# Time steps of the state-space layer with tokens on partitions, and their running sums as products with a triangle of ones

## The chip, the cores and the metric

The kernel runs on one core of a Trainium2 chip. The metric is the device time of one execution in microseconds. Before the change the median of three runs is 2298.25 us (2295.49 to 2298.49).

## The reference, cut to what matters

The program is a three-layer network on 512 tokens with 1024 features. The second layer's mixer is a state-space layer with 8 groups of 4 heads, so 32 heads. What the change touches is the step size of each token and head, and its running sum:

```
z, xbc, dt_raw = split(h @ w_in)                    # dt_raw: 512 tokens x 32 heads
dt = softplus(dt_raw + dt_bias)
a  = -exp(a_log)                                    # one value a head
cs = cumsum(dt * a) along the tokens                # inside a block of tokens
decay[l, s] = exp(cs[l] - cs[s]) for l >= s         # and, between blocks, with the block's end added
y  = (C B^T * decay) @ (x * dt) + d_skip * x
```

## The kernel before

All matrix products against weights are made in three parts: a weight chunk (128x1024) is loaded by SyncE into a ring of four buffers `raw`, ScalarE rounds it to `whi` (L1044), GpSimd takes `raw - whi` as `wlo` (L504), and TensorE multiplies `whi` and `wlo` with the high and low parts of the activations. One output tile is 24 products of 512 columns (L543, `single`). It goes to one of banks 0 to 3 in turn, so a tile waits until the tile four places before it has been read (`bank_free`).

The order of the work on each engine is written out by hand. In the state-space layer tile 0 of `m_in` holds `dt_raw` with the 32 heads on 32 partitions and the tokens along the free dimension. Tiles 1 to 4 are the x (two), B and C of group 0; VectorE runs a four-tap convolution over each (`conv(0, s)`, L1650 and L1652), ScalarE the silu (`conv_silu`, L1195). Tiles 5 and 6 are the gates of group 0. The first four tiles are computed together (`four("m_in", 2)`, L566 and L570), tiles 4 to 6 one after another in the loop at L807. Then `m_body(g)` computes for each group the six tiles of the next group, and between them turns x to token-major (`ssd_turn`), forms B times C (`ssd_cb`), and multiplies with the decays (`ssd_y`).

Before the first `m_body` VectorE works out the time steps (L1759 to L1784): bias, the exponent from ScalarE (L1186), a series for log(1+e), then the running sums of `-exp(a_log) * dt` by scans (L1780 inside each of four blocks of 128 tokens, L1782 from the end of a block over the rest), all as 32x512 tiles in SBUF with heads on partitions. `conv(0, 0)`, `conv(0, 1)` and `conv(0, 2)` stand between these operations. The result `cs` (32x1280) is written to memory (L468) and read back row by row, broadcast to 128 partitions, as `csb` (L463). SyncE does that after it has issued the load of chunk 12 of `m_in`, which itself waits until chunk 8 has been split. TensorE transposes `cs` and `dt` to token-major (L812, L813), VectorE copies these out as `cs_tok`, `ncs_tok`, `dt_tok` (L1876 to L1878), and all engines wait on `tok_ready` before the first `m_body`. `conv(0, 3)` comes after that wait.

A step wrapped in `step(...)` is waited for by VectorE itself before the next instruction.

Of the kernel before, what the change touches and what calls it, by code (L numbers as in the profile page):

```python
# [40 lines left out]
HEADS = GROUPS * HPG  # L41
# [45 lines left out]
T0, _ = starts(TILES)  # L87
# [36 lines left out]
def program(nc, io):  # L124
    with ExitStack() as ctx:
        def sem(name):
            return ctx.enter_context(nc.semaphore(name))

        def sb(name, shape, dt=F32):
            return ctx.enter_context(nc.sbuf_tensor(name, shape, dt))  # L130
# [13 lines left out]
        epscol = sb("epscol", [P, 1])  # L144
        dtp = sb("dtp", [HEADS, 4])
        acc = sb("acc", [P, S])
# [7 lines left out]
        ident = kst[:, K0["ident"]:K0["ident"] + P]  # L154
        tri = kst[:, K0["tri"]:K0["tri"] + P]
# [9 lines left out]
        def view(at, name, shape, dt=F32):  # L165
            with ExitStack() as v:
                if at:
                    v.enter_context(nc.sbuf_tensor(f"pad_{name}", [P, at // 4], F32))
                return v.enter_context(nc.sbuf_tensor(name, shape, dt))

        KB = 1024
        H = 0
        G = 32 * KB
# [25 lines left out]
        sums_m = view(G + 16 * KB, "sums_m", [P, 3, S])  # L199
        dts = view(G + 24 * KB, "dts", [HEADS, 7, S])  # L200
        cs = view(G + 76 * KB, "cs", [HEADS, PACK])
# [46 lines left out]

        dt_lin, dt_exp, a_exp, cs_ready, cs_out, tokT_done, tok_ready = (
            sem(n) for n in ("dt_lin", "dt_exp", "a_exp", "cs_ready", "cs_out", "tokT_done", "tok_ready"))  # L250
        grp_ready, xT_done, xdt_done, cb_done, cbm_dve, cbm_act = (
# [92 lines left out]
        def _(sp):  # L344
# [28 lines left out]
            sp.dma_start(kst[:], io["kst"]).then_inc(kst_in, 16)  # L373
            sp.dma_start(dtp[:, 0:2], io["dtp"]).then_inc(kst_in, 16)
            sp.dma_start(x[:], io["x"].rearrange("p (k n) -> p k n", k=KD)).then_inc(x_in, 16)
# [155 lines left out]
        def _(pe):  # L531
# [259 lines left out]
            def out_part(m, first, last):  # L791
# [12 lines left out]
                if last % CH == 0:  # L804
                    mm.then_inc(chunk_done, 1)

            for s in range(3, GSTEP):  # L807
                single("m_in", 1 + s, wait=False)

            pe.wait_ge(cs_ready, 1)  # L810
            for i in range(NT):
                nc.tensor.transpose(psum[4][:, i * HEADS:(i + 1) * HEADS], cs[:, i * P:(i + 1) * P], ident[0:HEADS, 0:HEADS])  # L812
                mm = nc.tensor.transpose(psum[5][:, i * HEADS:(i + 1) * HEADS], dts[:, 6, i * P:(i + 1) * P], ident[0:HEADS, 0:HEADS])  # L813
            mm.then_inc(tokT_done, 1)
            pe.wait_ge(tok_ready, 3)
            for g in range(GROUPS - 1):
# [218 lines left out]
        def _(act):  # L1035
# [147 lines left out]
            act.wait_ge(kst_in, 32)  # L1183
            nc.scalar.activation(dtp[:, 2:3], dtp[:, 1:2], ACT.Exp).then_inc(a_exp, 1)
            act.wait_ge(dt_lin, 1)
            nc.scalar.activation(dts[:, 1, :], dts[:, 0, :], ACT.Exp).then_inc(dt_exp, 1)  # L1186

# [74 lines left out]
            for s in range(GSTEP):  # L1262
# [4 lines left out]
                split_next(0, s)  # L1267
            act.wait_ge(tok_ready, 3)
            for g in range(GROUPS - 1):
# [211 lines left out]
        def _(dve):  # L1481
# [264 lines left out]
            def conv(G, s):  # L1746

                t = T0["m_in"] + 1 + GSTEP * G + s
                done(C0["m_in"] + 1 + GSTEP * G + s)
                if 4 * G + s >= 2:  # L1750

                    dve.wait_ge(grp_ready, 4 * G + s - 1)
                taps(tb[:, s % 2, :], psum[t % 4][:], "m_conv", 4 * G + s, 4, bank_free[t % 4])
# [3 lines left out]
            b = T0["m_in"] % 4  # L1757
            X, EXP, SERIES, SQUARE, SUM, MAX, DT = range(7)
            step(TS(dts[:, SUM, :], psum[b][0:HEADS, :], dtp[:, 0:1], None, ALU.add))  # L1759
            STT(out=dts[:, X, :], in0=dts[:, SUM, :], scalar=-1.0, in1=dts[:, SUM, :], op0=ALU.mult, op1=ALU.min).then_inc(dt_lin, 1)  # L1760
            TS(dts[:, MAX, :], dts[:, SUM, :], 0.0, None, ALU.max).then_inc(bank_free[b], 1)
            conv(0, 0)
            dve.wait_ge(dt_exp, 1)
            step(TS(dts[:, SERIES, :], dts[:, EXP, :], 2.0, None, ALU.add))
            step(nc.vector.reciprocal(dts[:, SERIES, :], dts[:, SERIES, :]))
            step(TT(dts[:, SERIES, :], dts[:, EXP, :], dts[:, SERIES, :], ALU.mult))
            conv(0, 1)
            step(TT(dts[:, SQUARE, :], dts[:, SERIES, :], dts[:, SERIES, :], ALU.mult))
            step(TS(dts[:, SUM, :], dts[:, SQUARE, :], 1.0 / 17, None, ALU.mult))
            for odd in range(15, 1, -2):  # L1770
                step(STT(out=dts[:, SUM, :], in0=dts[:, SUM, :], scalar=1.0 / odd, in1=dts[:, SQUARE, :], op0=ALU.add, op1=ALU.mult))
            step(STT(out=dts[:, SUM, :], in0=dts[:, SUM, :], scalar=1.0, in1=dts[:, SERIES, :], op0=ALU.add, op1=ALU.mult))
            step(STT(out=dts[:, DT, :], in0=dts[:, SUM, :], scalar=2.0, in1=dts[:, MAX, :], op0=ALU.mult, op1=ALU.add))
            dve.wait_ge(a_exp, 1)
            step(TS(dts[:, X, :], dts[:, DT, :], dtp[:, 2:3], -1.0, ALU.mult, ALU.mult))
            step(nc.vector.memset(dts[:, EXP, :], 1.0))

            for i in range(NT):
                at = slice(i * P, (i + 1) * P)
                step(nc.vector.tensor_tensor_scan(cs[:, at], dts[:, EXP, at], dts[:, X, at], 0.0, ALU.mult, ALU.add))  # L1780
            for i, (at, n) in OFF_COL.items():
                last = nc.vector.tensor_tensor_scan(cs[:, at:at + n], dts[:, EXP, (i + 1) * P:S], dts[:, X, (i + 1) * P:S],  # L1782
                                                    cs[:, (i + 1) * P - 1:(i + 1) * P], ALU.mult, ALU.add)
            last.then_inc(cs_ready, 1)  # L1784
            conv(0, 2)

# [86 lines left out]

            dve.wait_ge(tokT_done, 1)
            by_token = lambda bank: bank[:, 0:P].rearrange("p (i h) -> p i h", i=NT)
            nc.vector.tensor_copy(cs_tok[:], by_token(psum[4])).then_inc(tok_ready, 1)  # L1876
            TS(ncs_tok[:], by_token(psum[4]), -1.0, None, ALU.mult).then_inc(tok_ready, 1)
            nc.vector.tensor_copy(dt_tok[:], by_token(psum[5])).then_inc(tok_ready, 1)  # L1878
            dve.wait_ge(tok_ready, 3)
            conv(0, 3)  # L1880
# [251 lines left out]
def layout(a):  # L2132
# [14 lines left out]
    ins["kst"] = np.concatenate([np.eye(P), np.triu(np.ones((P, P))), qvalid, emask], axis=1).astype(np.float32)  # L2147
    ins["dtp"] = np.stack([a["m_dt_bias"][0], a["m_a_log"][0]], axis=1)
    ins["x"] = moving(a["x"][0].T)
# [56 lines left out]
```

## Time and profile before

| | before |
|---|---|
| median of 3 runs | 2298.25 us |
| profiled execution | 2297.04 us, its span 2295.2 us |
| TensorE busy | 2223.1 us, 97% |
| VectorE busy | 1242.6 us, 54% |
| ScalarE busy | 994.1 us, 43% |
| GpSimd busy | 974.2 us, 42% |
| mean granted TensorE clock | 0.978 |

The span is from the first to the last instruction that the profiler recorded. Busy shares are means over stages. Starts in the rows below are microseconds from the start of the span, and durations are microseconds unless marked ns. A matrix product's duration includes its way through the array, so products overlap; the distance between two starts is the rate.

### The profile page before, as it was taken

The page shows a single profiled execution, that of the slowest core. Times are in us where ns is not written, and L with a number is a line of the kernel's source. Part 1 is how long each engine was busy: PE and PEld are TensorE (multiplying, and loading weights), DVE is VectorE, ACT ScalarE, POOL GpSimd, SP SyncE. Part 2 cuts the span into 40 slices and gives each one's busy share as a digit, 9 for nine tenths or more (in the row PEclk, how much of TensorE's full clock was granted, in tenths as well). Part 3 has the DMA queues.
Part 4 walks back from the last instruction along what each step waited for, and adds up shares of the span by engine and source line. Part 5 has one row for each costly group of instructions (what it writes and reads, how often), then busy time and mean ns, then how long its engine had stood idle before and what let it go on. Part 6 is the DMA issues. An engine that isn't in the chain of part 4 may idle for free.

```text
span 2295.2 us, 28959 instructions
## 1 busy us (share of the span) xinstructions
PE 2223.1 (97%) x10434; PEld 1761.0 (77%) x10434; DVE 1242.6 (54%) x1718; ACT 994.1 (43%) x1420; POOL 974.2 (42%) x421
## 2 busy tenths in 40 slices
PE   6999999999979999989999999999999899999998
PEld 4788888788867777767788888878677688888886
DVE  5876666521297787786522221250777755666412
ACT  4324443333435546554534334453555634444332
POOL 3544443446534333334444446556211143444563
PEclk8999899999989999999899999999999999999999
DMA  7553475553315344332133223334321032333232
GB/s 304 212 202 125 152 265 201 185 143 95 115 40 186 111 142 149 113 111 90 59 103 97 91 72 95 109 106 145 97 67 47 29 107 76 108 93 91 76 91 72
DMA packets 74096, 273.83 MB, mean 119 GB/s; under 512 B 8519, under 2 KB 11207, under 8 KB 67736
## 3 DMA queue, kind: packets, MB, share of 16 engines
q1 hardware_dynamic: 70632, 266.74, 35.6%
q10 hardware_dynamic: 3376, 5.90, 0.8%
q8 instruction: 57, 0.93, 0.2%
q14 instruction: 31, 0.25, 0.0%
HBM read 269.21 MB, written 8.12 MB: 121 GB/s over the span
## 4 chain that ended last, share of the span: by engine, by line
PE 76%; issue 14%; POOL 5%; DVE 3%; ACT 1%; DMA 0%; ACTq 0%; POOLq 0%; SPq 0%; DVEq 0%
PE bank L543 60%; POOL wlo L504 5%; PE bank L913 4%; PE bank L566 2%; PE bank L1006 2%; PE bank L970 1%; PE bank L934 1%; PE bank L953 1%; PE bank L570 1%; PE bank L607 1%; PE bank L615 1%; PE bank L654 1%; PE bank L854 0%; DVE x L1553 0%; DMA ada_first<-ada_d 0%
## 5 line engine op out<-in xcount | busy, mean ns | idle before, releaser
L504 POOL TENSOR_TENSOR wlo<-raw,whi 128x1024 fp32r<-128x1024 f32 x382 | 928.8, 2438 | 1235.9 <-ACT whi L1044 1235.7
L1044 ACT ACTIVATE whi<-raw 128x1024 fp32r<-128x1024 f32 x382 | 401.3, 1055 | 622.9 <-PE bank L543 588.3
L543 PE MATMUL bank<-h_hi,whi 128*128 128x512 f32 x1616 | 649.3, 402 | 4.9 <-DVE dt_tok L1878 2.5
L543 PE MATMUL bank<-h_hi,wlo 128*128 128x512 f32 x1616 | 638.1, 395 | 0.0
L543 PE MATMUL bank<-h_lo,whi 128*128 128x512 f32 x1616 | 636.0, 394 | 0.0
L543 PEld LDWEIGHTS bank<-h_hi,whi 128*128 128x128 f32 x1616 | 303.9, 188 | 79.6 <-issue 5.7
L543 PEld LDWEIGHTS bank<-h_hi,wlo 128*128 128x128 f32 x1616 | 303.8, 188 | 77.2
L543 PEld LDWEIGHTS bank<-h_lo,whi 128*128 128x128 f32 x1616 | 304.0, 188 | 70.4
L543 PE MATMUL bank<-g_hi,whi 128*128 128x512 f32 x592 | 236.3, 399 | 0.0
L543 PE MATMUL bank<-g_hi,wlo 128*128 128x512 f32 x592 | 233.2, 394 | 0.0
L543 PE MATMUL bank<-g_lo,whi 128*128 128x512 f32 x592 | 232.1, 392 | 0.0
L1713 DVE TENSOR_TENSOR tb<-ta,bank 128x512 f32<-128x512 f32 x44 | 30.1, 685 | 222.3 <-PE bank L543 202.7
L1495 DVE TENSOR_TENSOR g_lo<-tb,g_hi 128x512 f32 (+1 forms) x52 | 109.1, 2098 | 51.9 <-ACT g_hi L1173 45.0
L543 PEld LDWEIGHTS bank<-g_hi,wlo 128*128 128x128 f32 x592 | 111.1, 188 | 29.1
L543 PEld LDWEIGHTS bank<-g_lo,whi 128*128 128x128 f32 x592 | 111.1, 188 | 26.4
L543 PEld LDWEIGHTS bank<-g_hi,whi 128*128 128x128 f32 x592 | 111.1, 188 | 25.4
L1511 DVE TENSOR_TENSOR sums<-sums,sq 128x512 f32<-128x512 f32 x21 | 14.5, 692 | 193.2 <-ACT sq L1107 193.1
L1652 DVE SCALAR_TENSOR_TENSOR tb<-bank,vec,tb 128x511 f32<-128x511 f32 (+1 forms) x140 | 104.8, 749 | 9.8
L566 PE MATMUL bank<-h_hi,whi 128*128 128x512 f32 x160 | 68.2, 426 | 9.2 <-ACT h_hi L1089 7.0
L1843 DVE TENSOR_TENSOR csb<-csb,cbm 128x1280 f32<-128x1280 f32 x32 | 72.0, 2288 | 0.3
L519 POOL TENSOR_TENSOR h_lo<-tb,h_hi 128x512 fp32r<-128x512 f32 x35 | 45.2, 1293 | 59.9 <-ACT tb L1090 59.6
L566 PE MATMUL bank<-h_hi,wlo 128*128 128x512 f32 x160 | 67.2, 420 | 0.0
(337 smaller groups left out, 2953.5 us busy)
## 6 DMA issues: line engine op xcount, KB each, us to landing
raw<-f_in_d SPq DMA_DIRECT2D x88, 512.0 KB, 3.5
raw<-m_d SPq DMA_DIRECT2D x65, 512.0 KB, 3.7
ada_f<-ada_d SPq DMA_DIRECT2D x24, 1024.0 KB, 7.0
raw<-g_in_d SPq DMA_DIRECT2D x44, 512.0 KB, 3.5
raw<-w_in_d SPq DMA_DIRECT2D x41, 512.0 KB, 3.6
csb<-cs_d SPq DMA_DIRECT2D x32, 640.0 KB, 6.5
ada_a<-ada_d SPq DMA_DIRECT2D x16, 1024.0 KB, 4.9
raw<-a_in_d SPq DMA_DIRECT2D x24, 512.0 KB, 6.0
```

The costliest lines, as they stand in the source:

```text
L504: nc.gpsimd.tensor_tensor(wlo[:, s], raw[:, s], whi[:, s].bitcast(F32), ALU.subtract).then_inc(lo_ready, 1)
L519: nc.gpsimd.tensor_tensor(h_lo[:, k, :], tb[:, k % 2, :], h_hi[:, k, :].bitcast(F32), ALU.subtract).then_inc(in_ready, 1)
L543: mm = nc.tensor.matmul(psum[bank][:], w[:, s, kk, :], xs[part == "lo"][:, k, :], start=first and kk == 0 and i == 0, stop=last and kk == ...
L566: nc.tensor.matmul(psum[tiles[i]][:], w[:, (C0[name] + i) % RING, k, :], h_hi[:, k, :], start=k == 0 and j == 0, stop=False)
L570: mm = nc.tensor.matmul(psum[tiles[i]][:], whi[:, (C0[name] + i) % RING, k, :], h_lo[:, k, :], start=False, stop=k == KD - 1)
L913: mm = nc.tensor.matmul(psum[7][:], w[:, c % RING, m // 3, :], (h_hi, h_lo)[part == "lo"][:, m // 3, :], start=m == 0, stop=m == 23)
L1006: mm = nc.tensor.matmul(psum[b][:], w[:, c % RING, k, :], (h_hi, h_lo)[part == "lo"][:, k, :], start=kk == 0 and i == 0, stop=kk == 3 and ...
L1044: nc.scalar.activation(whi[:, s], raw[:, s], ACT.Copy).then_inc(hi_ready, 1)
L1495: TT(dst, whole, hi.bitcast(F32), ALU.subtract).then_inc(in_ready, 1)
L1652: ins = STT(out=out[:, d:S], in0=src[:, 0:S - d], scalar=col(width - 1 - d), in1=out[:, d:S], op0=ALU.mult, op1=ALU.add)
L1713: TT(tb[:, j % 2, :], ta[:, j % 2, :], psum[b][:], ALU.mult).then_inc(bank_free[b], 1)
L1843: TT(csb[:, r, :], csb[:, r, :], cbm[:], ALU.mult).then_inc(m_done, 1)
```

## The change

The 32x512 product `dt_raw` is copied out of its bank at once and turned by four transposes to 128 tokens by 4x32 (block, head), all before tile 4. Bias, exponent, series and the product with `-exp(a_log)` are then made on 128x128 tiles, with one operand of each in PSUM in most of them; `dt_tok` is now their direct result. For that the parameters `dtp` are loaded broadcast to 128 partitions. The running sums are five fp32 products with the triangle of ones `tri`, issued after tile 5: one gives `cs` with tokens on partitions, four give it with heads on partitions. The sums from a block's end over later blocks are the in-block sums plus the end, or plus two or three ends that are added first. The whole series stands between `conv(0, 0)` and `conv(0, 1)`, where it stood on both sides of `conv(0, 1)`. The transposes at L812 and L813 and the copies at L1876 to L1878 go away, and the wait for the token-major values comes before `conv(0, 2)`.

```diff
-        dtp = sb("dtp", [HEADS, 4])
+        dtp = sb("dtp", [P, 2, HEADS])
...
-        dts = view(G + 24 * KB, "dts", [HEADS, 7, S])
+        dts = view(G + 24 * KB, "dts", [HEADS, S])
+        dtt = view(G + 26 * KB, "dtt", [P, 6, NT, HEADS])
+        ends = view(G + 29 * KB, "ends", [HEADS, 4])
...
-            sp.dma_start(dtp[:, 0:2], io["dtp"]).then_inc(kst_in, 16)
+            sp.dma_start(dtp[:].rearrange("p a h -> p (a h)"), io["dtp"].broadcast_to([P, 2 * HEADS])).then_inc(kst_in, 16)
...
+            b = T0["m_in"] % 4
+            pe.wait_ge(bank_free[b], T0["m_in"] // 4 + 1)
+            for i in range(NT):
+                mm = nc.tensor.transpose(psum[4][:, i * HEADS:(i + 1) * HEADS], dts[:, i * P:(i + 1) * P], ident[0:HEADS, 0:HEADS])
+            mm.then_inc(dt_turn, 1)
             for s in range(3, GSTEP):
                 single("m_in", 1 + s, wait=False)
-
+                if s == 4:
+                    pe.wait_ge(dta_out, 1)
+                    nc.tensor.matmul(psum[4][:, P:2 * P], tri, dtt[:, 5].rearrange("p i h -> p (i h)"), start=True, stop=True)
+                    for i in range(NT):
+                        mm = nc.tensor.matmul(psum[5][0:HEADS, i * P:(i + 1) * P], dtt[:, 5, i, :], tri, start=True, stop=True)
+                    mm.then_inc(cs_sum, 1)
+            pe.wait_ge(tok_ready, 2)
             pe.wait_ge(cs_ready, 1)
-            for i in range(NT):
-                nc.tensor.transpose(psum[4][:, i * HEADS:(i + 1) * HEADS], cs[:, i * P:(i + 1) * P], ident[0:HEADS, 0:HEADS])
-                mm = nc.tensor.transpose(psum[5][:, i * HEADS:(i + 1) * HEADS], dts[:, 6, i * P:(i + 1) * P], ident[0:HEADS, 0:HEADS])
-            mm.then_inc(tokT_done, 1)
-            pe.wait_ge(tok_ready, 3)
...
-            nc.scalar.activation(dtp[:, 2:3], dtp[:, 1:2], ACT.Exp).then_inc(a_exp, 1)
+            nc.scalar.activation(psum[6][:, 0:HEADS], dtp[:, 1, :], ACT.Exp).then_inc(a_exp, 1)
             act.wait_ge(dt_lin, 1)
-            nc.scalar.activation(dts[:, 1, :], dts[:, 0, :], ACT.Exp).then_inc(dt_exp, 1)
+            nc.scalar.activation(psum[5][:, P:2 * P], dtt[:, 0].rearrange("p i h -> p (i h)"), ACT.Exp).then_inc(dt_exp, 1)
...
-            step(TS(dts[:, SUM, :], psum[b][0:HEADS, :], dtp[:, 0:1], None, ALU.add))
-            STT(out=dts[:, X, :], in0=dts[:, SUM, :], scalar=-1.0, in1=dts[:, SUM, :], op0=ALU.mult, op1=ALU.min).then_inc(dt_lin, 1)
-            TS(dts[:, MAX, :], dts[:, SUM, :], 0.0, None, ALU.max).then_inc(bank_free[b], 1)
+            nc.vector.tensor_copy(dts[:], psum[b][0:HEADS, :]).then_inc(bank_free[b], 1)
...
+            dve.wait_ge(dt_turn, 1)
+            linear = by_head(psum[4][:, 0:P])
+            step(TT(SUM_P, linear, bias, ALU.add))
+            step(TT(SUM, linear, bias, ALU.add))
+            step(TS(MAX_P, SUM, 0.0, None, ALU.max))
+            STT(out=X, in0=SUM_P, scalar=-1.0, in1=SUM, op0=ALU.mult, op1=ALU.min).then_inc(dt_lin, 1)
             conv(0, 0)
             dve.wait_ge(dt_exp, 1)
+            step(TS(DENOM, EXP_P, 2.0, None, ALU.add))
+            step(nc.vector.reciprocal(DENOM, DENOM))
+            step(TT(SERIES, EXP_P, DENOM, ALU.mult))
+            step(nc.vector.tensor_copy(SER_P, SERIES))
+            SQUARE_P = SUM_P
+            step(TT(SQUARE_P, SER_P, SERIES, ALU.mult))
+            step(TS(SUM, SQUARE_P, 1.0 / 17, None, ALU.mult))
+            for odd in range(15, 1, -2):
+                step(STT(out=SUM, in0=SUM, scalar=1.0 / odd, in1=SQUARE_P, op0=ALU.add, op1=ALU.mult))
+            step(STT(out=SUM, in0=SUM, scalar=1.0, in1=SER_P, op0=ALU.add, op1=ALU.mult))
+            step(STT(out=dt_tok[:], in0=SUM, scalar=2.0, in1=MAX_P, op0=ALU.mult, op1=ALU.add))
+            dve.wait_ge(a_exp, 1)
+            rate = psum[6][:, 0:HEADS].unsqueeze(1).broadcast_to([P, NT, HEADS])
+            STT(out=DTA, in0=rate, scalar=-1.0, in1=dt_tok[:], op0=ALU.mult, op1=ALU.mult).then_inc(dta_out, 1)
             conv(0, 1)
...
-            for i in range(NT):
-                at = slice(i * P, (i + 1) * P)
-                step(nc.vector.tensor_tensor_scan(cs[:, at], dts[:, EXP, at], dts[:, X, at], 0.0, ALU.mult, ALU.add))
+            dve.wait_ge(cs_sum, 1)
+            nc.vector.tensor_copy(cs_tok[:], by_head(psum[4][:, P:2 * P])).then_inc(tok_ready, 1)
+            TS(ncs_tok[:], by_head(psum[4][:, P:2 * P]), -1.0, None, ALU.mult).then_inc(tok_ready, 1)
+            step(nc.vector.tensor_copy(cs[:, 0:S], psum[5][0:HEADS, :]))
+            end = [cs[:, (i + 1) * P - 1:(i + 1) * P] for i in range(3)] + [ends[:, i:i + 1] for i in range(3)]
+            for i, (a, c) in enumerate(((0, 1), (1, 2), (3, 2))):
+                step(TS(end[3 + i], end[a], end[c], None, ALU.add))
             for i, (at, n) in OFF_COL.items():
-                last = nc.vector.tensor_tensor_scan(cs[:, at:at + n], dts[:, EXP, (i + 1) * P:S], dts[:, X, (i + 1) * P:S],
-                                                    cs[:, (i + 1) * P - 1:(i + 1) * P], ALU.mult, ALU.add)
+                for j in range(i + 1, NT):
+                    first = {(0, 1): 0, (1, 2): 1, (2, 3): 2, (0, 2): 3, (1, 3): 4, (0, 3): 5}[i, j]
+                    col = at + (j - i - 1) * P
+                    last = TS(cs[:, col:col + P], cs[:, j * P:(j + 1) * P], end[first], None, ALU.add)
+                    if (i, j) != (1, 3):
+                        step(last)
             last.then_inc(cs_ready, 1)
+            dve.wait_ge(tok_ready, 2)
             conv(0, 2)
```

## Rows read from the trace of the kernel before

**Rows 1.** The page: busy time, share of the span, instructions.
```profile
PE 2223.1 (97%) x10434; PEld 1761.0 (77%) x10434; DVE 1242.6 (54%) x1718; ACT 994.1 (43%) x1420; POOL 974.2 (42%) x421
```

**Rows 2.** TensorE's waits, 640 to 760 us: total, times, longest.
```profile
PE bank L812 <- DVE cs L1782: 8.4, 1, 8.4
PE bank L543 <- DVE dt_tok L1878: 2.5, 1, 2.5
PE bank L543 <- DVE dts L1761: 1.0, 1, 1.0
```

**Rows 3.** Timeline of TensorE: start, duration, instruction, idle before and its releaser.
```profile
658.20 0.50 PE L543 MATMUL bank<-h_hi,whi 128*128 128x512 f32 x1 [1.05 <-DVE dts L1761]
...
687.21 0.79 PE L543 MATMUL bank<-h_hi,whi 128*128 128x512 f32 x1 [2.53 <-DVE dt_tok L1878]
...
694.59 1.03 PE L734 MATMUL bank<-kst,xg 128*128 128x128 f32 x8
...
714.56 2.39 PE L768 MATMUL bank<-csb,xdt 128*64 128x128 f32 x28
...
779.72 1.12 PE L727 MATMUL bank<-sq,ones 128*128 128x512 f32 x2 [0.55 <-DVE sq L1801]
```

**Rows 4.** Stretches: length, PE, PEld, DVE, ACT, POOL busy, then PEclk, DMA.
```profile
675.30:683.60 8.30, 0.00 (x0) 0.00 (x0) 7.79 (x15) 0.00 (x0) 0.00 (x0) 0.62 0.14 55
...
687.20:691.10 3.90, 3.89 (x10) 3.07 (x11) 2.99 (x4) 1.84 (x4) 2.38 (x1) 0.53 0.00 0
...
1809.00:1812.00 3.00, 1.78 (x18) 1.28 (x18) 2.93 (x7) 2.69 (x7) 0.00 (x0) 0.74 0.00 0
```

**Rows 5.** Timeline of VectorE.
```profile
654.17 0.74 DVE L1759 TENSOR_SCALAR dts<-bank,dtp 32x512 f32<-32x512 f32 x1 [2.42 <-PE bank L570]
...
658.08 0.73 DVE L1650 TENSOR_SCALAR tb<-bank,vec 128x512 f32<-128x512 f32 x1
...
665.92 0.75 DVE L1650 TENSOR_SCALAR tb<-bank,vec 128x512 f32<-128x512 f32 x1
...
668.94 0.67 DVE L1768 TENSOR_TENSOR dts<-dts 32x512 f32<-32x512 f32 x1
...
686.48 0.28 DVE L1876 COPY cs_tok<-bank 128x128 f32<-128x128 f32 x1
686.68 0.28 DVE L1877 TENSOR_SCALAR ncs_tok<-bank 128x128 f32<-128x128 f32 x1
...
705.65 3.50 DVE L1843 TENSOR_TENSOR csb<-csb,cbm 128x1280 f32<-128x1280 f32 x2
```

**Rows 6.** Single lines: durations in ns, shortest/median/longest, first and last start.
```profile
L1652 DVE SCALAR_TENSOR_TENSOR tb<-bank,vec,tb x140: 746/748/752, 658.8 to 2161.6; 128x511 f32<-128x511 f32 x54, 128x510 f32<-128x510 f32 x54, 128x509 f32<-128x509 f32 x32
...
L1652 DVE SCALAR_TENSOR_TENSOR tb<-ta,vec,tb x16: 749/750/2771, 61.6 to 180.5; 128x511 f32<-128x511 f32 x8, 128x510 f32<-128x510 f32 x8
...
L1828 DVE TENSOR_SCALAR csb<-csb,cs_tok x128: 269/277/589, 699.2 to 1008.0; 128x128 f32<-128x128 f32 x128
...
L1979 DVE TENSOR_SCALAR stat<-stat x48: 168/169/2331, 1614.9 to 1810.1; 128x2 f32<-128x2 f32 x48
...
L1765 DVE RECIPROCAL dts<-dts x1: 3341/3341/3341, 661.5 to 661.5; 32x512 f32<-32x512 f32 x1
...
L741 PE MATMUL bank<-cg,bg x64: 271/275/275, 701.1 to 1007.2; 128*128 128x128 f32 x64
```

**Rows 7.** Timeline of GpSimd.
```profile
655.36 2.51 POOL L504 TENSOR_TENSOR wlo<-raw,whi 128x1024 fp32r<-128x1024 f32 x1 [5.03 <-ACT whi L1044]
...
670.80 2.95 POOL L504 TENSOR_TENSOR wlo<-raw,whi 128x1024 fp32r<-128x1024 f32 x1 [5.46 <-ACT whi L1044]
```

**Rows 8.** Timeline of SyncE's queue.
```profile
691.12 0.43 SPq L468 DMA_DIRECT2D cs_d<-cs  x1
694.95 2.00 SPq L463 DMA_DIRECT2D csb<-cs_d  x4
```

**Rows 9.** Timeline of ScalarE, first decay row of group 0.
```profile
699.20 1.31 ACT L1211 ACTIVATE csb<-csb,ncs_tok 128x384 f32<-128x384 f32 x3 [1.96 <-DMA csb<-cs_d]
```

More of the change, by code:

```diff
@@ L247, in program @@
         gate_out, prod_out, conv_out = sem("gate_out"), sem("prod_out"), sem("conv_out")
-        dt_lin, dt_exp, a_exp, cs_ready, cs_out, tokT_done, tok_ready = (
-            sem(n) for n in ("dt_lin", "dt_exp", "a_exp", "cs_ready", "cs_out", "tokT_done", "tok_ready"))
+        dt_turn, dt_lin, dt_exp, a_exp, dta_out, cs_sum, cs_ready, cs_out, tok_ready = (
+            sem(n) for n in ("dt_turn", "dt_lin", "dt_exp", "a_exp", "dta_out", "cs_sum", "cs_ready", "cs_out", "tok_ready"))
         grp_ready, xT_done, xdt_done, cb_done, cbm_dve, cbm_act = (
@@ L469, in _ @@
             sp.wait_ge(cs_out, 16)
-            sp.wait_ge(tok_ready, 3)
+            sp.wait_ge(tok_ready, 2)
             for f in range(2):
@@ L1267, in _ @@
                 split_next(0, s)
-            act.wait_ge(tok_ready, 3)
+            act.wait_ge(tok_ready, 2)
             for g in range(GROUPS - 1):
@@ L1757, in _ @@
             b = T0["m_in"] % 4
-            X, EXP, SERIES, SQUARE, SUM, MAX, DT = range(7)
-            step(TS(dts[:, SUM, :], psum[b][0:HEADS, :], dtp[:, 0:1], None, ALU.add))
-            STT(out=dts[:, X, :], in0=dts[:, SUM, :], scalar=-1.0, in1=dts[:, SUM, :], op0=ALU.mult, op1=ALU.min).then_inc(dt_lin, 1)
-            TS(dts[:, MAX, :], dts[:, SUM, :], 0.0, None, ALU.max).then_inc(bank_free[b], 1)
+            nc.vector.tensor_copy(dts[:], psum[b][0:HEADS, :]).then_inc(bank_free[b], 1)
+            by_head = lambda t: t.rearrange("p (i h) -> p i h", i=NT)
@@ new lines, in _ @@
+            SUM_P, EXP_P, SER_P, MAX_P = (by_head(psum[5][:, i * P:(i + 1) * P]) for i in range(4))
+            X, SUM, SERIES, DENOM, DT, DTA = (dtt[:, i] for i in range(6))
+            bias = dtp[:, 0, :].unsqueeze(1).broadcast_to([P, NT, HEADS])
+            dve.wait_ge(dt_turn, 1)
[4 more added lines that the diff above has]
+            STT(out=X, in0=SUM_P, scalar=-1.0, in1=SUM, op0=ALU.mult, op1=ALU.min).then_inc(dt_lin, 1)
@@ L1762, in _ @@
             conv(0, 0)
             dve.wait_ge(dt_exp, 1)
-            step(TS(dts[:, SERIES, :], dts[:, EXP, :], 2.0, None, ALU.add))
-            step(nc.vector.reciprocal(dts[:, SERIES, :], dts[:, SERIES, :]))
-            step(TT(dts[:, SERIES, :], dts[:, EXP, :], dts[:, SERIES, :], ALU.mult))
-            conv(0, 1)
[L1768 to L1776, printed above, removed]
-            for i in range(NT):
-                at = slice(i * P, (i + 1) * P)
-                step(nc.vector.tensor_tensor_scan(cs[:, at], dts[:, EXP, at], dts[:, X, at], 0.0, ALU.mult, ALU.add))
@@ L1872, in mixed @@
                     lo_part(m_lo[:, k, :], y32[:, k, :], m_hi[:, k, :], I0["m_out"] + k)
[L1874 to L1879, printed above, removed]
             conv(0, 3)
@@ L2147, in layout @@
     ins["kst"] = np.concatenate([np.eye(P), np.triu(np.ones((P, P))), qvalid, emask], axis=1).astype(np.float32)
-    ins["dtp"] = np.stack([a["m_dt_bias"][0], a["m_a_log"][0]], axis=1)
+    ins["dtp"] = np.concatenate([a["m_dt_bias"][0], a["m_a_log"][0]])[None]
     ins["x"] = moving(a["x"][0].T)
```

## The prediction, made before the changed kernel was built or run

> **What bounds the kernel now.** I read the page first. TensorE is busy 97% of the span and the others about half [rows 1], so over the whole kernel time is won only where TensorE stands still or runs slowly. The second view is TensorE's waits in the stretch that the change touches: 8.4 us for the last scan of the running sums, then 2.5 us for the copy of `dt_tok`, and 1.0 us earlier for the bank that L1761 frees [rows 2]. The third is TensorE's timeline. Tile 4 starts at 658.20, three tiles of 24 products follow at one product per 0.233 us (a tile is 5.7 us with its first gap), and they are through at 675.1. Then TensorE has only eight small transposes until 687.21, when the first tile of `m_body(0)` starts. That tile ends at 694.59 and the next begins behind the eight transposes of `ssd_turn`, at 695.4 [rows 3]. The stretches tell the rest: in 675.3 to 683.6 the mean granted clock is 0.62, which means the clock fell to 1.2 GHz about 2 us after TensorE had stopped, and until 691.1 it is 0.53 [rows 4]. Nine products there start 0.43 us apart instead of 0.233, so the low level costs 1.7 us after the wait. The hole is about 12 us of missing work and 1.7 us of slow work, and VectorE is what ends it: its series and scans run without a pause.
>
> I use one mark for the sum, the start of the second tile of `m_body(0)`: 695.4 before.
>
> **Step 1, bank and turn.** The copy of `dt_raw` takes the place of L1759 at 654.17 (0.74 us) [rows 5], so the bank is free at 654.9 rather than after L1761. Tile 4 then waits only for GpSimd's chunk, which ends at 657.87 [rows 7], and starts at 657.9, 0.3 us earlier. The four transposes issue after TensorE's last product of the four tiles (657.0) at 0.13 us each, as the eight at 694.59 [rows 3]. They lie inside that same wait and cost nothing; without that cover, 0.5 us. VectorE gets their result at 657.7.
>
> **Step 2, the 128x128 operations.** The trace has copies out of PSUM of this size at 0.28 us [rows 5] and a scalar operation in SBUF of 0.277 [rows 6]; with the 0.04 us that a waited step adds, I take 0.32 us each. Bounds: 0.20 us, the start distance of the two copies at 686.48 with no wait between, and 0.75 us, the 512-wide forms. The reciprocal of 512 elements takes 3.34 us [rows 6]; a quarter and the fixed part of the 2-wide operations (0.17) give 0.98. Four operations end at 659.0. `conv(0, 0)` takes its 3.0 us, to 662.0, 0.9 us later than before. Then 16 operations, 15 at 0.32 and the reciprocal: 5.8 us, to 667.8. None of them reads two SBUF tensors. Such forms never lengthened in 140 cases (746 to 752 ns), where the form with two SBUF inputs goes to 2771 [rows 6], so GpSimd's pieces beside them cost nothing; if they do count, that is a rival below. ScalarE's exponent (0.3 us) and the chunk behind it come 2 us later; chunk 5 is then split at 662.8, and tile 5 needs it at 663.6.
>
> A rule that speaks against the step is in the Trainium skill, VectorE: DVE Perf Modes, section "The TRN2 errata": a PSUM source costs 62 cycles more of fixed part than an SBUF one. By that the series would be an estimated 1 us longer. The trace has no such difference at this size (0.28 against 0.277), so the sum doesn't hold it.
>
> **Step 3, conv(0, 1) behind the whole series.** Before, it ran at 665.92 to 668.94 [rows 5], just in time for tile 6, which takes its bank. Now it runs 667.8 to 670.8. TensorE ends tile 5 at 669.2, makes the five fp32 products (ten records, as L741's are two records each [rows 6], 1.3 us at 0.13) until 670.5 and starts tile 6 at 670.9. The products lie in the wait for the bank; uncovered they cost 1.3 us. Tile 6 ends at 676.6, 1.5 us later than before.
>
> **Step 4, the sums out of PSUM.** After 670.8: two copies (0.2 each), the 32x512 copy (0.74), three sums of ends (0.20 each) to 672.6, and six 32x128 additions (0.31 each): 674.4 if nothing else happens. But these nine are scalar operations with input and output in SBUF. Such operations stretch when GpSimd is in a piece: L1979 from 169 to 2331 ns, L1828 from 277 to 589 [rows 6]. GpSimd's next piece starts 1.86 us after `conv(0, 1)` ends (668.94 to 670.80 before [rows 5, 7]), so at 672.7, for 2.4 us. I let one addition pass; five wait to 675.2 and end at 676.8. Bounds of this wait: 0 and 2.4 us, and I take the upper one, because the piece is released by the same `conv(0, 1)` as the additions.
>
> **Step 5, the start of m_body(0).** Its first tile takes the bank of `conv(0, 2)`, which is now queued behind the additions on VectorE: 676.8 to 679.8. So TensorE waits 3.2 us, 676.6 to 679.8. The old gap shows the clock falling after about 2 us, the sparse work of 1809 to 1812 lowers it too (0.74) [rows 4]; I take the fall and the same 1.7 us. Bounds: 0 and 1.7, or 4.7 if a whole tile runs slowly. First tile 679.8 to 687.2, transposes 0.8, mark at 688.0. Gain at the mark: 7.4 us. `conv(0, 3)` and its silu are done at 683.5, chunk 8 at 684.0, both in time.
>
> **Step 6, the decay rows.** They don't gain as much. `cs` is written once load 12 has gone, and that waits for chunk 8: 690.72 before, when `cs` had long been ready, and 684.0 now. 0.4 us on, the write's 3.8 us and 4.2 us to the first row [rows 8, 9] put it at 692.4, 4.4 us behind the mark, before 3.8. The first group has the room: the products that need its first decays began at 714.56, those decays were done at 709.1 [rows 3, 5]. ScalarE and VectorE run 0.6 us later against TensorE through group 0, and the square sum of that group, which already misses by 0.55 us in later groups [rows 3], can miss by 0.3 in the first: cost 0.3 us. Bounds: 0 and 2.4, one GpSimd piece in front of it.
>
> Nothing else moves: the broadcast of `dtp` is 32 KB at the start in the shadow of the first loads.
>
> **Sum.** 7.4 - 0.3 = 7.1 us. The profiled execution of 2297.04 us (span 2295.2 and 1.8 around it) becomes 2289.9. The median of the runs is 1.2 us above the profiled one, so 2291.1 is the median I forecast. What is late next is `conv(0, 2)`, that is VectorE behind GpSimd.
>
> **Rivals.**
> The additions escape GpSimd (0.18): `conv(0, 2)` ends at 677.4, TensorE waits 0.8 us, the clock stays, mark at 684.0, which is 11.4 us earlier. The rows then lag 2.4 us more and cost about 1.2 at the first square sum. 10.2 us gained, 2288.0. For it: half of a 2 us interval decides. Against: both start from one event.
>
> The clock stays high in a wait of 3.2 us (0.17): mark 9.1 us earlier, lag 2.3 us, cost 1.2: 2290.3, the same answer.
>
> Late pieces add up (0.17): the square sum meets a full piece (2.4), the low clock lasts two more products (0.4): gain 4.6, 2293.6.
>
> The series waits for GpSimd in spite of its PSUM operands (0.08): the pieces for chunks 5 and 6 lie in it, up to 2.2 us each, gain 2.7, 2295.5. Against it are 140 rows without one case.
>
> The lag of group 0 stays (0.06): if VectorE can't regain the 2.4 us, each of seven groups repeats it, 16.8 us against 9.1 gained, 7.7 us slower: 2306. It decides from 1.3 us a group. For it: TensorE already waits on VectorE once a group [rows 3]. Against: VectorE is busy about 33 us of each 43 us group, so it has 10 us to catch up.
>
> **How the numbers follow.** My forecast has 0.34. With the rival that gives the same time it holds half. A measurement of this kernel can tell about 0.2% (4.6 us) from no change. Faster by more than that: the forecast, the two next to it and the first rival, and half of the late pieces, 0.79; within it: 0.14; slower: 0.07. The range reaches from 2285.5 (first rival, and no cost at the square sum) to 2295.5.
>
> **What would show it.** In the profile after: four transposes before 658 and tile 4 at 657.9; series of 128x128 operations at 0.32 us without a 2 us one; tile 6 at 670.9 behind a wait for `conv(0, 1)`; one addition of over 2 us, beside a GpSimd piece; TensorE's wait of about 3 us for `conv(0, 2)` with a clock under 1.0 behind it; the mark near 688; no new wait after the first square sum. The forecast is wrong if the series takes over 8 us, if the additions don't stretch, or if any group after the second starts with a larger wait than 0.55 us.

## The result: 39.8 us faster, about four fifths of it outside the changed code

The changed kernel takes 2258.55 us (median of 4 runs, 2257.73 to 2260.74) against 2298.37 us for the kernel before (4 runs). The ratio is 0.9832, with a 95% interval of 0.9819 to 0.9844. The forecast was 2291.1 with a range of 2285.5 to 2295.5, so the result is 27 us below the range. The profiled execution has a span of 2255.9 us against 2295.2. In the spans, that is 39.3 us less. One execution of e12 below took 2447.12 us at a mean granted clock of 0.84; it moves that median by 0.01 us, and no other was slow.

I read the profile after in the same order. First the busy line, then TensorE's waits from 630 to 1110 us, which is the whole state-space stage and more than the stretch of [rows 2], as total, times, longest:

```profile
PE 2185.6 (97%) x10440; PEld 1758.1 (78%) x10440; DVE 1229.8 (55%) x1722; ACT 993.5 (44%) x1420; POOL 975.6 (43%) x421
```

```profile
PE bank L729 <- DVE sq L1827: 11.7, 6, 6.7
PE bank L545 <- DVE tb L1660: 3.3, 2, 3.0
PE bank L545 <- POOL wlo L506: 1.8, 2, 1.4
```

In the kernel before, the square sums (L727 there) waited as follows between the same times:

```profile
PE bank L727 <- DVE sq L1801: 8.9, 6, 6.3
```

The wait of 8.4 us for the scans and that of 2.5 us for `dt_tok` [rows 2] are gone, and the forecast wait of about 3 us for `conv(0, 2)` has come (L1660). The square sums wait 2.8 us more in all. The busy line holds the surprise: TensorE has six more instructions than before, and is busy 37.5 us less (2185.6 against 2223.1 [rows 1]). Waits that go away don't make the work itself shorter.

TensorE's timeline of the stage: the four transposes, tile 4, the products with the triangle, tile 6, the first tile of `m_body(0)`, the transposes behind it, and the square sum of group 1:

```profile
648.48 0.43 PE L812 MATMUL bank<-kst,dts 32*128 32x32 f32 x4
649.34 0.47 PE L545 MATMUL bank<-h_hi,whi 128*128 128x512 f32 x1 [0.42 <-POOL wlo L506]
...
660.41 0.38 PE L818 MATMUL bank<-dtt,kst 128*128 128x128 f32 x2
660.72 1.06 PE L820 MATMUL bank<-kst,dtt 128*32 128x128 f32 x8
662.03 0.50 PE L545 MATMUL bank<-h_hi,whi 128*128 128x512 f32 x1 [0.24 <-DVE tb L1660]
...
670.83 0.47 PE L545 MATMUL bank<-h_hi,whi 128*128 128x512 f32 x1 [3.03 <-DVE tb L1660]
...
676.41 1.04 PE L736 MATMUL bank<-kst,xg 128*128 128x128 f32 x8
...
761.04 1.12 PE L729 MATMUL bank<-sq,ones 128*128 128x512 f32 x2 [1.00 <-DVE sq L1827]
```

Tile 4 starts at 649.34 and not at 658.20 [rows 3]. Of these 8.86 us, 8.56 are won before the first changed instruction of the series: the copy of `dt_raw` starts at 645.61 (below), and the instruction in its place started at 654.17 [rows 5]. That is the part that my prediction does not have. It becomes visible when one reads the distance between starts of products in a place without waits. The mean over all neighbouring 512-column products (some 7950 distances between 205 and 260 ns) is 233.4 ns before and 229.0 ns after, in every stage of the program alike. A stage that the change doesn't touch shows it in two rows: from the first sums after the short convolution to the sums after the first feed-forward block there are 1584 such products. The first block is the kernel before, the second the kernel after.

```profile
226.88 2.73 PE L607 MATMUL bank<-ones,sums 128*128 128x1 f32 x24
...
623.12 2.73 PE L607 MATMUL bank<-ones,sums 128*128 128x1 f32 x24
```

```profile
225.48 2.74 PE L609 MATMUL bank<-ones,sums 128*128 128x1 f32 x24
...
615.06 2.73 PE L609 MATMUL bank<-ones,sums 128*128 128x1 f32 x24
```

396.24 us against 389.58: 6.66 us less, or 4.2 ns for each of 1584 products.

Inside the stage of the series things went almost as forecast. VectorE's timeline after (the copy of `dt_raw`, the first of the four operations, the seven terms of the series, the sums, `conv(0, 2)`), then GpSimd's piece, SyncE's queue and ScalarE's first decay row:

```profile
645.61 0.68 DVE L1766 COPY dts<-bank 32x512 f32<-32x512 f32 x1 [2.10 <-PE bank L572]
648.95 0.30 DVE L1773 TENSOR_TENSOR bank<-bank,dtp 128x128 f32<-128x128 f32 x1 [2.67 <-PE bank L812]
...
653.47 0.95 DVE L1780 RECIPROCAL dtt<-dtt 128x128 f32<-128x128 f32 x1
...
655.78 2.21 DVE L1787 SCALAR_TENSOR_TENSOR dtt<-dtt,bank 128x128 f32<-128x128 f32 x7
...
658.88 0.74 DVE L1658 TENSOR_SCALAR tb<-bank,vec 128x512 f32<-128x512 f32 x1
...
664.01 2.62 DVE L1806 TENSOR_SCALAR cs<-cs,ends 32x128 f32<-32x128 f32 x2
666.66 0.59 DVE L1806 TENSOR_SCALAR cs<-cs 32x128 f32<-32x128 f32 x2
...
667.49 0.73 DVE L1658 TENSOR_SCALAR tb<-bank,vec 128x512 f32<-128x512 f32 x1
```

```profile
663.76 2.48 POOL L506 TENSOR_TENSOR wlo<-raw,whi 128x1024 fp32r<-128x1024 f32 x1 [6.32 <-ACT whi L1052]
```

```profile
675.17 0.43 SPq L470 DMA_DIRECT2D cs_d<-cs  x1
679.13 1.98 SPq L465 DMA_DIRECT2D csb<-cs_d  x4
```

```profile
683.27 1.31 ACT L1219 ACTIVATE csb<-csb,ncs_tok 128x384 f32<-128x384 f32 x3 [3.81 <-DMA csb<-cs_d]
```

And the granted clock behind TensorE's wait (length, busy of PE, PEld, DVE, ACT, POOL, then PEclk, DMA):

```profile
667.00:671.20 4.20, 1.17 (x6) 0.69 (x5) 4.06 (x7) 0.59 (x1) 0.00 (x0) 1.00 0.41 125
671.20:675.00 3.80, 3.80 (x18) 3.13 (x17) 2.28 (x4) 2.46 (x5) 2.42 (x1) 1.00 0.00 0
```

It stayed at 2.4 GHz, where the longer hole of before had lowered it [rows 4]. That is so in this execution; in most later ones of the same series it fell, as the section on the prediction shows.

### The profile page after: what moved, and what is told of

Same layout as the page of the kernel before. It is cut to its first block, busy times and chain, and to the rows that moved or that the text cites. A ratio compares the mean times of both kernels' runs of the same rounds, so it can differ in the third digit from the quotient of the medians.

```text
span 2255.9 us, 28975 instructions
## 1 busy us (share of the span) xinstructions
PE 2185.6 (97%) x10440; PEld 1758.1 (78%) x10440; DVE 1229.8 (55%) x1722; ACT 993.5 (44%) x1420; POOL 975.6 (43%) x421
## 4 chain that ended last, share of the span: by engine, by line
PE 76%; issue 14%; POOL 5%; DVE 3%; ACT 1%; DMA 0%; ACTq 0%; POOLq 0%; SPq 0%; DVEq 0%
PE bank L545 60%; POOL wlo L506 5%; PE bank L921 4%; PE bank L568 2%; PE bank L1014 2%; PE bank L978 1%; PE bank L942 1%; PE bank L572 1%; PE bank L961 1%; PE bank L656 1%; PE bank L617 1%; PE bank L609 1%; PE bank L862 1%; DVE x L1561 0%; DMA x<-x_d 0%
## 5 line engine op out<-in xcount | busy, mean ns | idle before, releaser
L545 PE MATMUL bank<-h_hi,whi 128*128 128x512 f32 x1616 | 639.7, 396 | 5.1 <-DVE tb L1660 3.3
L545 PE MATMUL bank<-g_hi,whi 128*128 128x512 f32 x592 | 230.9, 390 | 0.0
L1660 DVE SCALAR_TENSOR_TENSOR tb<-bank,vec,tb 128x511 f32<-128x511 f32 (+1 forms) x140 | 104.9, 749 | 9.8
L568 PE MATMUL bank<-h_hi,whi 128*128 128x512 f32 x160 | 67.5, 422 | 8.9 <-ACT h_hi L1097 7.0
```

Of the source, the lines that this page charges most:

```text
L545: mm = nc.tensor.matmul(psum[bank][:], w[:, s, kk, :], xs[part == "lo"][:, k, :], start=first and kk == 0 and i == 0, stop=last and kk == ...
L568: nc.tensor.matmul(psum[tiles[i]][:], w[:, (C0[name] + i) % RING, k, :], h_hi[:, k, :], start=k == 0 and j == 0, stop=False)
L1660: ins = STT(out=out[:, d:S], in0=src[:, 0:S - d], scalar=col(width - 1 - d), in1=out[:, d:S], op0=ALU.mult, op1=ALU.add)
```

## What moved without being named in the change

`dtp` grew from 4 to 64 floats a partition (16 to 256 bytes). SBUF addresses are handed out in the order of the tensors, and a tensor takes a multiple of 32 bytes in this program. So every tensor behind `dtp` moved up by 224 bytes: `acc` from 86848 to 87072, and all views with the moving operands of the large products (`h_hi`, `h_lo`, `g_hi`, `g_lo`, `m_hi`, `mg_hi` and so on) from 105440 to 105664. Modulo 256 the views go from 224 to 192. The weights `whi` and `wlo` are allocated earlier and stay at 128. Within these tensors all steps are multiples of 512 bytes, so one number holds for all products.

Each large product has two operands in SBUF: a block of weights (`whi` or `wlo`), which a weight load of its own (PEld in the profile) brings in, and 512 columns of activations, here called the moving operand. Theory A: the start address of the moving operand sets the pace. Theory B: something in the changed code does. Theory C came up after the first runs: the distance between moving operand and weights, modulo 256, sets it.

## The experiments

**Moving the tiles by 32 or 64 bytes.** Four kernels, each one line in front of `acc`:

```diff
+        sb("gap", [P, 8])       # e1, e3: 32 bytes
+        sb("gap", [P, 16])      # e2, e4: 64 bytes
         acc = sb("acc", [P, S])
```

> The kernel before with an unused tensor of 32 bytes a partition in front of acc and nothing else: all later tiles lie 32 bytes higher, so that the moving operands of the large products (h_hi, g_hi and the rest) start at a multiple of 64 bytes instead of 32 above one, as they do in the changed kernel. Theory A (the start address of the moving operand sets the pace of the products: 0.233 us a product before, 0.229 after): about 30 us faster than before, near 2268, products 0.229 us apart everywhere. Theory B (the 30 us outside the stretch of the series come from something in the changed code itself): the same time as before, 2298, products 0.233 apart.

> The kernel before with an unused tensor of 64 bytes a partition in front of acc: all later tiles move by 64 bytes, the moving operands still start 32 above a multiple of 64. Theory A in its form with 64-byte multiples: the same as before, 2298, products 0.233 us apart. If any move of the tiles or a multiple of 128 or 256 were what counts, it would be 10 to 30 us faster. Theory B: the same.

> The changed kernel with an unused tensor of 32 bytes a partition in front of acc: the moving operands start 32 bytes above a multiple of 64 again. Theory A: the 30 us are lost and only the gain of the series is left, 9 us against before: 2289, products 0.233 us apart. Theory B: 2258.5 as the changed kernel.

> The changed kernel with an unused tensor of 64 bytes a partition in front of acc: the moving operands start at a multiple of 256 bytes instead of at 192 above one. Theory A with 64-byte multiples: 2258.5, as the changed kernel. If larger multiples count further: faster than that, at most by another 30 us (products 0.225 us apart). Theory B: 2258.5.

Measured (kernel before beside them: 2296.67 us): e1 2290.47 (ratio 0.9961 to 0.9982), e2 2301.86 (1.0017 to 1.0040), e3 2290.64 (0.9966 to 0.9985), e4 2281.24 (0.9914 to 0.9948). The brackets are 95% intervals of the ratio to it. Theory B falls: an unused tensor of 32 bytes takes 32 of the 40 us back (e3), and the old program gets slower with one of 64 bytes, where theory A too had expected no change. Theory A holds in its kind but not in its form: multiples of 64 bytes are not the rule, since e1 has one and gains 6 us only, and e4 has one and is 23 us slower than the changed kernel. The paces pair up across the two programs: 233.4 ns for before and e3, both at 224; 232.6 and 232.4 for e1 and e4, both at 0.

**Which address.** e5 moves only the weights, e6 only the second region of views, e7 only the scratch tiles, and e8 all later tiles by 128 bytes.

```diff
+        csil = sb("csil", [P, KD])          # e5: 32 bytes, moved here from behind mod
         raw = sb("raw", [P, RING, CH, P])
...
-        G = 32 * KB                         # e6
+        G = 32 * KB + 32
...
+        ssum = sb("ssum", [P, NT])          # e7: 32 bytes, moved here from behind root
         acc = sb("acc", [P, S])
...
+        sb("gap", [P, 32])                  # e8
         acc = sb("acc", [P, S])
```

> The changed kernel with the 32-byte tensor csil moved in front of raw: raw, whi, wlo and x lie 32 bytes higher, everything from ncol on (all moving operands) stays. Theory A (the pace of a product follows from the start address of the moving operand alone; so far 233.35 ns at 224 modulo 256, 229.0 at 192, 232.4 at 0, 234.25 at 32, in either kernel): 229.0 ns a product and 2258. Theory C (it follows from the distance between the moving operand and the weights that are loaded meanwhile): another pace, 230 to 234, and 2265 to 2300. Theory B (no address matters): 2258.

> The changed kernel with only the second region of views moved up by 32 bytes (G = 32 KB + 32): h_hi and h_lo stay at 192 modulo 256, g_hi, g_lo, m_lo, mg_hi and mg_lo go to 224. Theory A: inside one execution products with h_hi and h_lo stay at 229.0 ns and products with g_hi, g_lo and mg go to 233.35, so about 2400 slower products by 4.4 ns, 10 us: 2268. Theory B (one pace for a whole program, set by anything but the operand's address): all products alike.

> The kernel before with ssum (32 bytes) moved in front of acc: acc, modacc, sq, rstd, ta, tb and root lie 32 bytes higher, the views with the moving operands of the large products stay at 224 modulo 256. Theory A: 233.35 ns a product and 2297, the kernel before. If the place of the scratch tiles, which VectorE, ScalarE and GpSimd use, were the cause: 232.4 ns and 2290 as in the gap of 32 bytes.

> The changed kernel with an unused tensor of 128 bytes a partition in front of acc: the moving operands start at 64 modulo 256, which is 64 modulo 128 as in the changed kernel. Theory A with a period of 128 bytes: 229.0 ns, 2258. With a period of 256 bytes or with the distance to the weights modulo 256 as its argument: another pace between 228 and 235 ns, and about 7.8 us for each ns.

Measured: e5 2290.95, e6 2269.24, e7 2298.75 (one run), e8 2291.05 us. e7 leaves the pace at 233.4: the scratch tiles have no part in it. e6 shows the address most clearly, because it has both paces in one execution. Twice two starts 24 products apart, first with `h_hi` (192 modulo 256), then with `g_hi` (224):

```profile
2024.71 0.39 PE L545 MATMUL bank<-h_hi,whi 128*128 128x512 f32 x1
...
2030.20 0.39 PE L545 MATMUL bank<-h_hi,whi 128*128 128x512 f32 x1
...
2134.70 0.39 PE L545 MATMUL bank<-g_hi,whi 128*128 128x512 f32 x1
...
2140.30 0.39 PE L545 MATMUL bank<-g_hi,whi 128*128 128x512 f32 x1
```

5.49 and 5.60 us, 229 and 233 ns a product; the means over the execution are 229.1 with `h` and 233.3 with `g`. But e5 refutes theory A: no moving operand moved, only the weights by 32 bytes, and the pace went from 229.0 to 233.3 and 32 us were lost. e8 (233.3 ns) rules out a period of 128 bytes. Theory C had allowed both paces, but had no value of its own for either distance yet, so it needed a test.

**The distance.** e9 gives the kernel before the distance 64 by moving the weights instead of the views, e10 tries the distance 0. e11 belongs to the stage of the series (below), e12 is the changed kernel again.

```diff
+        csil = sb("csil", [P, KD])          # e9, in the kernel before
         raw = sb("raw", [P, RING, CH, P])
...
+        sb("gap", [P, 48])                  # e10, in the changed kernel
         acc = sb("acc", [P, S])
```

> The kernel before with the 32-byte tensor csil moved in front of raw, no instruction changed: the weights whi and wlo start at 160 modulo 256, the moving operands stay at 224, so their distance is 64 as in the changed kernel (192 and 128). Theory C (the pace follows from that distance modulo 256: 64 gives 229.0 ns, 96 gives 233.35, 128 gives 232.4, 160 gives 234.25, 32 and 192 give 233.3): 229.0 ns and 2297 less 30, so 2267, without any part of the change. Theory A (the moving operand's address alone): 233.35 and 2297. A third form, in which both addresses count by themselves: another pace.

> The changed kernel with an unused tensor of 192 bytes a partition in front of acc: moving operands and weights both start at 128 modulo 256, distance 0, which no run had. Theory C has no value for it; the values so far lie between 229.0 and 234.25 ns, so 2258 to 2297; below 229.0 it would be a faster kernel than the changed one, by 7.8 us for each ns. Theory A: a value of its own for the address 128.

Measured (kernel before beside them: 2298.01): e9 2268.58 (ratio 0.9856 to 0.9889), e10 2248.59 (0.9765 to 0.9804). e9 has no changed instruction, the moving operands at their old addresses, and the pace of the changed kernel, 229.0 ns. Its two rows for the feed-forward block stand 389.6 us apart like those after. So addresses alone give 29.4 us, of the 36.8 that the changed kernel gains beside the same runs (e12 below, 2261.19). e10 is faster than the changed kernel by 10 us, at 226.7 ns with `g` and 227.3 with `h`. That is less than my 7.8 us for each ns. The state-space stage is why: between the sums before and behind it (the rows of L607 or L609) it takes 468.54 us in e10 and 465.35 after. The granted clock fell behind TensorE's wait in e10 and not after, and the first tile of `m_body(0)` took 8.31 us instead of 5.58.

**Distance 0 at another address, the missing distance, and both gains together.**

```diff
+        sb("gap0", [P, 8])                  # e15, in the kernel before
         raw = sb("raw", [P, RING, CH, P])
...
+        sb("gap", [P, 40])                  # e15 and e14 (e14 in the changed kernel)
         acc = sb("acc", [P, S])
```

> The kernel before with unused tensors of 32 bytes in front of raw and 160 bytes in front of acc, no instruction changed: weights and moving operands both start at 160 modulo 256, distance 0. Theory C: 226.8 ns a product as at 128 and 128, and a time near the changed kernel without any of its instructions, 2297 less 30 less 10, so 2258. If the absolute addresses count besides the distance: another pace.

> The changed kernel with a gap of 160 bytes in front of acc: moving operands at 96, weights at 128 modulo 256, distance 224, the one multiple of 32 that no run had. Theory C has no value for it; the other odd multiples of 32 gave 233.3 (32), 233.35 (96) and 234.25 (160), so 233 to 234.5 ns and 2288 to 2297 are likely if the pattern holds.

Measured (kernel before beside them: 2296.16): e15 2252.64 (0.9793 to 0.9823), e14 2289.92 (0.9961 to 0.9981). e15 has weights and moving operands at 160 where e10 has them at 128, and the same pace to 0.1 ns: the distance decides, not the place. It is also 6 us faster than the changed kernel, and has not one of its changed instructions.

All runs in one table, but for e6, which has the distances 64 and 96 in one program (229.1 and 233.3 ns; 2269.24 us). Distance is the address of the moving operand less that of the weights, modulo 256; the pace is the mean time between starts, over all large products of the one profiled execution of each:

| distance | pace, ns | kernels (median us) |
|---|---|---|
| 0 | 227.2 | e10 (2248.59), e15 (2252.64), e13 (2242.88) |
| 32 | 233.3 | e5 (2290.95) |
| 64 | 229.0, e12 229.5 | after (2258.55), e9 (2268.58), e11 (2258.85), e12 (2261.19) |
| 96 | 233.4 | before, e3 (2290.64), e7 (2298.75) |
| 128 | 232.4 to 232.6 | e4 (2281.24), e1 (2290.47) |
| 160 | 234.3 | e2 (2301.86) |
| 192 | 233.3 | e8 (2291.05) |
| 224 | 233.3 | e14 (2289.92) |

**The gain of the series by itself.** Pairs with equal distance differ in the series and not in the pace:

> The changed kernel once more on the chip that runs e9 and e11: 2258.5, 229.0 ns a product. Against e9, which has the same pace and the old series, it gives the gain of the series alone: 7.1 us by the forecast, 9 us by the marks in the profile after. Against e11 it gives the price of the wait for conv(0, 2).

e12 measured 2261.19 (0.9816 to 0.9855), so 7.4 us less than e9, measured beside it. The other pairs measured side by side give 9.2 (e1 less e4) and 6.0 (before less e3); e15 less e10, not side by side, gives 4.1. The forecast was 7.1. The traces allow a closer look, at the state-space stage alone, from the sums in front of it to those behind it:

| distance | old series, us | new series, us | gain | first tile of `m_body(0)`, new series |
|---|---|---|---|---|
| 96 | before 477.52 | e3 471.31 | 6.2 | 7.22 us |
| 128 | e1 480.05 | e4 472.60 | 7.5 | 8.43 us |
| 0 | e15 475.89 | e10 468.54 | 7.4 | 8.31 us |
| 64 | e9 475.05 | after 465.35, e12 465.49 | 9.7, 9.6 | 5.58 us, 5.60 us |

The series gains most where its first tile is not slowed by a lower clock. Two microseconds of a single stage are scatter, though: e7 took 479.85 with the distance and the series of before.

**The wait for conv(0, 2).** e11 takes away what forms it, by another order of the instructions:

```diff
             step(nc.vector.tensor_copy(cs[:, 0:S], psum[5][0:HEADS, :]))
+            dve.wait_ge(tok_ready, 2)
+            conv(0, 2)
             ...
             last.then_inc(cs_ready, 1)
-            dve.wait_ge(tok_ready, 2)
-            conv(0, 2)
...
             pe.wait_ge(tok_ready, 2)
-            pe.wait_ge(cs_ready, 1)
```

> The changed kernel with conv(0, 2) in front of the sums of ends and the six additions, and without TensorE's wait for cs_ready (tok_ready stays; the decay rows still wait for cs_ready). No tile moves. If the additions behind GpSimd's piece are what keeps TensorE waiting 3.03 us before m_body(0): conv(0, 2) starts at 663.0 instead of 667.5, that wait is gone, and the time is 3 us below the changed kernel, 2255.5. If the decay rows or the square sum of group 0 take over: 0 to 1 us below it.

Measured 2258.85 (4 runs, 2254.47 to 2264.41), 2.3 us below e12, measured beside it, with ranges that overlap: not told apart by the times. The trace shows what happened. TensorE's waits in e11 from 620 to 760 us, of 0.4 us and more:

```profile
PE bank L568 <- ACT h_hi L1096: 1.8, 1, 1.8
PE bank L736 <- ACT cg L1202: 1.2, 1, 1.2
PE bank L729 <- DVE sq L1826: 0.7, 1, 0.7
PE bank L545 <- POOL wlo L506: 0.4, 1, 0.4
```

The 3.0 us are gone and 1.2 come back one step later: `conv(0, 3)` is now the one behind the additions, which met GpSimd's next piece instead (one pair took 2.72 us at 668.48), and `ssd_turn` waits for its silu. Another 0.7 us come back at the first square sum. The stage takes 464.23 us, 1.1 less than after.

> The changed kernel with both findings: the gap of 192 bytes (distance 0, 226.8 ns a product) and conv(0, 2) in front of the additions without the wait for cs_ready. If the two gains add: 2248.6 of the gap alone less 2 to 3 us, 2246. If the faster products leave the wait of the state-space stage as it is (the square sum of each group): 2248.6.

e13 measured 2242.88 us (5 runs, 2239.61 to 2245.21; ratio 0.9748 to 0.9775): faster than before and after by 53 and 16 us, and 5.7 below e10, which was not measured beside it. The two gains add, and by more than the 2 to 3 us that I had expected: the stage takes 464.81 us and e10's 468.54, because without the wait the clock stays up, too.

## Why the prediction was wrong

**The step that failed is the last sentence of the working, "Nothing else moves".** I had the broadcast of `dtp` there as 32 KB of transfer and had not asked what its 240 more bytes do to the addresses behind it. Some 7950 products became 4.3 ns shorter, 34 us if all of them bound the time; e9 shows 29.4 of it reaching the end. No rival had it either: all of mine lie in the stage of the series. The trace of before could not have told it, as all its large products have one distance and one pace, 233 ns.

The other steps can be judged apart from it. The table has the kernel after, with 8.56 us added so that the copy of `dt_raw` lies at its old place, and e3, the same program back at the distance of before, with 1.99 us taken off for the same reason:

| | forecast | after | e3 |
|---|---|---|---|
| steps 1, 2: transposes seen by VectorE | 657.7 | 657.5 | 657.6 |
| four operations done, `conv(0, 0)` starts | 659.0 | 658.7 | 658.8 |
| series done, `conv(0, 1)` starts | 667.8 | 667.4 | 667.5 |
| step 3: tile 6 starts | 670.9 | 670.6 | 670.6 |
| step 4: GpSimd's piece starts | 672.7 | 672.3 | 672.4 |
| additions done, `conv(0, 2)` starts | 676.8 | 676.0 | 676.3 |
| step 5: TensorE's wait, then `m_body(0)` | 3.2 us, 679.8 | 3.03 us, 679.4 | 3.17 us, 679.7 |
| mark, second tile | 688.0 | 685.8 | 687.7 |
| step 6: `cs` written, first decay row | 684.4, 692.4 | 683.7, 691.8 | 684.0, 692.2 |
| wait at the square sum of group 0 | 0.3 us | 0 | 0.64 us |

**Steps 1 to 4 were right.** The 0.32 us for an operation was 0.32 to 0.33, the reciprocal 0.95 of length where I had 0.98 with its step. No operation of the series lengthened beside GpSimd's pieces at 651.60 and 655.03, so the rival with PSUM operands is out. The rule of the Trainium skill on a dearer PSUM source (VectorE: DVE Perf Modes, "The TRN2 errata") would have made the series an estimated 1 us longer; its 16 operations took 5.72 us (653.16 to 658.88), and the sum without the rule has 5.8. One addition waited for GpSimd, as foreseen:

```profile
L1806 DVE TENSOR_SCALAR cs<-cs x3: 274/275/276, 663.7 to 667.0; 32x128 f32<-32x128 f32 x3
L1806 DVE TENSOR_SCALAR cs<-cs,ends x3: 274/275/2309, 664.0 to 667.3; 32x128 f32<-32x128 f32 x3
```

**Step 5 had one term that failed in the kernel after, and not in e3.** I took 1.7 us for a lower clock behind the wait. After, it stayed at its upper level (1.00 in both stretches above), as the rival "The clock stays high" (0.17) has it, and the mark gained 9.6 us and not 7.4: 0.4 because VectorE was done sooner, 1.8 in the first tile and its transposes. In e3 it fell, and nine products ran at the lower level, as in the hole of before. The stretches, with columns as above:

```profile
678.40:682.40 4.00, 0.83 (x4) 0.67 (x4) 3.86 (x7) 0.95 (x2) 0.00 (x0) 1.00 0.28 114
682.40:685.80 3.40, 3.40 (x9) 2.67 (x9) 1.96 (x3) 2.06 (x4) 2.38 (x1) 0.50 0.00 0
```

The mark of e3 gained 7.7 us, and the start of the first square sum 7.0, where the forecast had 7.1 in all. Of the nine profiled executions that have this wait, the clock stayed up in three (after, e6, e12: waits of 3.02 and 3.03 us, first tile 5.6 us) and fell in six (e3, e5, e8, e14: 3.16 and 3.17 us, 7.2 us; e4 and e10: 3.17 and 3.05 us, 8.4 and 8.3 us). What decides it is open. That the kernel after kept its clock is luck as far as these runs tell; that e3 meets the forecast so closely is in part luck too, as its additions ended 0.5 us sooner than forecast and its square sum waited 0.3 us longer.

**Step 6 was right in kind.** After, the first decay row came 6.1 us behind the mark instead of 4.4, as it does when the clock stays, and the square sum of group 0 cost nothing. From group 1 on it waits 1.0 us instead of 0.55. I had named that as a sign that the forecast is wrong, but it does not come from the series: e9, with the old series and the new pace, waits 1.0 us as well, and e3, with the new series and the old pace, 0.55. TensorE's faster products come to the square sum sooner and VectorE doesn't, so a group takes 43.28 us after and 43.34 before. That is why the state-space stage profits least from the pace, 2.5 us (before less e9).

**Two numbers of the prediction do not follow from its own terms.** "The first rival, and no cost at the square sum" gives 2286.8 and not 2285.5, and the chances of its rivals add up to 0.775, 0.165 and 0.06 for faster, within and slower, where it has 0.79, 0.14 and 0.07. Neither would have changed the outcome.

The Trainium skill says in SBUF — State Buffer, section "SBUF: two separate sides", that among the engines only the port pair shared by VectorE and GpSimd causes contention, and that TensorE never waits on anyone there. For VectorE's 2309 ns beside GpSimd the traces agree with it. No run here shows TensorE waiting on another engine's access to SBUF; what they show is a pace that depends on the places of its own two operands, 229.0 or 233.3 ns for the same products when the weights move by 32 bytes (after, e5).

**What is still open.** Why the distance counts. Weight loads run beside the products all the time (3.13 us busy of 3.80 in the second stretch above), so a conflict of the two reads is a reading that suggests itself, but no run here looks at the reads. The pace is also not fixed by the distance alone. In e12, the same program as after at the same addresses, the second half of the first feed-forward block ran at 233.3 ns a product and everything else at 229.0, which cost 3.5 us (393.12 us between its two rows of sums, 389.58 after); in e1 the second feed-forward block ran at 233.3 and the rest near 232.4. No run tells what changed there. And all distances here are of fp32r products of 512 columns; others were not tried.

## What to carry to other kernels

A change in the size of one small tensor moves everything allocated behind it; compare the addresses of both programs before you assign a gain or loss to the code, and repeat a surprising result with an unused tensor of the same size in the old kernel. When TensorE bounds the time, read the distance between starts of its products in a quiet place as a number of its own: waits and busy shares don't show it. Here it costs an unused tensor to try a distance between weights and moving operand, and the best of eight (0) with the reordering of one convolution took another 16 us off, where the new series had given 4 to 9.

## What the runs showed of the hardware that I had not expected

The pace of back-to-back products of 512 columns with 128x128 weights, at a granted clock of 1.00, depends on the distance of their two SBUF addresses modulo 256 bytes: 227.2 ns at 0, 229.0 at 64, 232.4 to 234.3 at the other six multiples of 32. It is the same at two absolute places for 0 (e10, e15) and for 64 (after, e9), but for stretches of e12 and e1. A wait of TensorE of 3.02 or 3.03 us between two full tiles left the granted clock at its upper level in three executions; behind one of 3.05 to 3.17 us it fell to 0.50 in six, where the hole of 8.3 us had a mean of 0.62 [rows 4].
